# Moving the arena of a two-block transformer kernel by 128 bytes in every SBUF partition

## The reference

```python
# first block, depth 2
x = x + window_gqa_sink(h, w_qkv_a, w_out_a, sink_a)       # layer 0: windowed attention
x = x + dilated_mixture_attention(h, w_qkv_b, w_out_b)     # layer 1: three dilated groups
x = x + swiglu(h, w_gate, w_up, w_down)                    # after each: 1024 -> 2816 -> 1024
# second block, depth 2, on x (512 tokens) and a context y (256 tokens)
f_in, f_gate, g_u, g_v, g_gate, c_q, c_kv, k_rope, a_gate = _split_in(h @ w_in)
x = x + gate * (jnp.concatenate([fx, gx, ox], axis=-1) @ w_out[l])
```

## The kernel before, in words

| tile | address before | past a multiple of 256 |
|---|---|---|
| `w_lo`, `w_hi`, `x`, `y`, `ident`, `ones` | 16,512 (`w_lo`), 32,896 (`w_hi`) ... | 128 |
| `rows`, `sq` | 76,480 and 81,600 | 192 |
| first tile of the arena (`h_hi` and others) | 87,744 | 192 |
| all moving and stationary fp32r activation tiles (`h`, `a`, `b`, `f0m`, `f1m`, `l_hx`, `l_hy`, `l_h`, `l_m`, each `_hi` and `_lo`) | in the arena | 192 |
| `l_tm`, `l_gu`, `l_fg` | in the arena | 128 |

## Time and profile before

### The profile page before, as it was taken

How to read it: one execution, slowest core, us unless ns; L and a number is a source line. 1 busy time by engine, 2 the same in 40 slices (tenths; PEclk the granted TensorE clock), 3 DMA queues, 4 the chain that set the end, 5 groups by cost and what they waited for, 6 DMA issues and landing times.

```text
span 2251.5 us, 31279 instructions
## 1 busy us (share of the span) xinstructions
PE 2217.8 (99%) x13114; PEld 1795.1 (80%) x13114; DVE 998.9 (44%) x1519; ACT 832.7 (37%) x1291; POOL 735.1 (33%) x339
## 2 busy tenths in 40 slices
PE   9999999999999999999999999999999999999999
PEld 7778888888889888888778888887885667886677
DVE  5655555621222232223366555445204673541672
ACT  6544333233233343334453333333224432333531
POOL 3116444455432332323164444443220101332102
PEclk9999999999999999999999999999999999999999
DMA  4113444432322222122034444433110001322002
GB/s 147 40 47 112 140 141 147 152 103 94 116 84 67 67 66 75 66 73 68 30 103 144 150 147 141 134 100 122 57 65 33 1 1 38 131 75 80 1 1 75
DMA packets 54587, 193.36 MB, mean 86 GB/s; under 512 B 6832, under 2 KB 8112, under 8 KB 53552
## 3 DMA queue, kind: packets, MB, share of 16 engines
q1 hardware_dynamic: 43056, 153.72, 20.8%
q10 hardware_dynamic: 11392, 37.65, 4.4%
HBM read 189.24 MB, written 2.10 MB: 85 GB/s over the span
## 4 chain that ended last, share of the span: by engine, by line
PE 88%; DVE 3%; ACT 1%; issue 1%; DVEq 0%; DMA 0%; POOL 0%; POOLq 0%
PE ps L174 21%; PE ps L176 20%; PE ps L175 20%; PE ps L2523 4%; PE ps L177 3%; PE ps L179 3%; PE ps L178 3%; PE ps L2555 2%; PE ps L1052 2%; PE ps L1078 2%; PE ps L2535 2%; PE ps L1063 1%; PE ps L1919 1%; DVE dvS L1111 0%; DMA w_raw<-in_wstream 0%
## 5 line engine op out<-in xcount | busy, mean ns | idle before, releaser
L246 POOL TENSOR_TENSOR w_lo<-w_raw,w_hi 128x1024 fp32r<-128x1024 f32 x282 | 681.7, 2419 | 1390.4 <-ACT w_hi L164 1390.4
L174 PE MATMUL ps<-h_hi,w_hi 128*128 128x512 f32 x1168 | 469.9, 402 | 4.6 <-DVE w_lo L288 2.1
L164 ACT ACTIVATE w_hi<-w_raw 128x1024 fp32r<-128x1024 f32 x284 | 299.4, 1057 | 438.0 <-DMA w_raw<-in_wstream 436.7
L176 PE MATMUL ps<-h_hi,w_lo 128*128 128x512 f32 x1168 | 458.1, 392 | 0.0
L175 PE MATMUL ps<-h_lo,w_hi 128*128 128x512 f32 x1168 | 454.6, 389 | 0.0
L174 PEld LDWEIGHTS ps<-h_hi,w_hi 128*128 128x128 f32 x1168 | 219.5, 188 | 52.4 <-issue 4.0
L176 PEld LDWEIGHTS ps<-h_hi,w_lo 128*128 128x128 f32 x1168 | 219.3, 188 | 50.9
L175 PEld LDWEIGHTS ps<-h_lo,w_hi 128*128 128x128 f32 x1168 | 219.6, 188 | 45.5 <-issue 0.7
L1255 ACT ACTIVATE sq<-sq,dnm 128x768 f32<-128x768 f32 x64 | 59.4, 930 | 184.3 <-DVE dnm L1161 184.3
L177 PE MATMUL ps<-w_hi,h_hi 128*128 128x256 f32 x416 | 117.0, 281 | 3.2 <-DVE dvS L1111 3.2
L178 PE MATMUL ps<-w_lo,h_hi 128*128 128x256 f32 x416 | 115.2, 277 | 0.0
(11 more groups left out here) (323 smaller groups left out, 4141.0 us busy)
## 6 DMA issues: line engine op xcount, KB each, us to landing
w_raw<-in_wstream SPq DMA_DIRECT2D x283, 512.0 KB, 3.4
f0mod_rows<-in_wmod ACTq DMA_DIRECT2D x24, 512.0 KB, 4.2
f1mod_rows<-in_wmod ACTq DMA_DIRECT2D x24, 512.0 KB, 4.5
l_dft<-in_dft ACTq DMA_DIRECT2D x4, 1024.0 KB, 6.9
out<-x SPq DMA_DIRECT2D x8, 256.0 KB, 3.6
x<-in_x SPq DMA_DIRECT2D x3, 512.0 KB, 7.0
l_wuq<-in_wuq ACTq DMA_DIRECT2D x2, 768.0 KB, 6.7
dist<-in_dist ACTq DMA_DIRECT2D x1, 1152.0 KB, 6.4
```

Of the source, the lines that this page charges most:

```text
L164: self.A.activation(self.w_hi[:, n % RING, :], self.w_raw[:, n % RING, :], ACT.Copy).then_inc(self.w_high, 1)
L174: T.matmul(out, wh, ah, start=start, stop=False)
L176: return T.matmul(out, wl, ah, start=False, stop=stop)
L246: G.tensor_tensor(c.w_lo[:, n % RING, :], c.w_raw[:, n % RING, :], c.w_hi[:, n % RING, :].bitcast(F32), ALU.subtract).then_inc(c.w_low, 1)
```

## The change

The arena begins 128 bytes later: at 87,872 in place of 87,744, which is 64 past a multiple of 256. Everything placed by `ctx`, or at a sum of arena offsets, moves by the same 128 bytes: the fp32r activation tiles go from 192 to 64 past a multiple of 256, `l_tm`, `l_gu` and `l_fg` from 128 to 0. What is allocated ahead of the arena (the ring of weights, `x`, `y`, `rows`, `sq`) stays. No instruction is added, removed, reshaped or moved in the order of any engine, and no wait changes.

```diff
-        self.top = self.offset = (nc.sbuf_base + 31) // 32 * 32
+        self.top = self.offset = (nc.sbuf_base + 31) // 32 * 32 + 128
```

## The result

The changed kernel is slower: 2276.33 us median of 4 runs (2275.58 to 2279.34) against 2251.4 us (with one run more than in the table above), a ratio of 1.0112 (95% interval 1.0095 to 1.013), or 25 us. The profiled execution took 2276.8 us with a span of 2275.5 us, 24.0 us more than before. The forecast, no change, was wrong; the time is where the slower rival put it.

The account below looks back on a forecast made before the run. TensorE's pace from one matmul to the next was taken to bound the kernel, not waits or data transfers. Six terms of 0 left the span at 2251.5 us, forecast 2251.2 us, range 2226 to 2281.

Parts of the forecast that it names:

- the slower rival: Moving slices at 64 past 256 fall to the pace of those at 128: 27.2 us, 2278.4 us; chance 0.25.
- Items 1 to 4: Orders and waits, other engines on arena tiles, DMAs landing in the arena, plain fp32 matmuls: each taken as 0.
- item 4: Plain fp32 matmuls, 0.430 us from start to start: change taken as 0.
- Item 5: 512-column fp32r matmuls moving from the arena, 1984 triples: taken as no change; upper bound 0.700 us a triple.
- block "kr": Stationary slices start at 128 and 0 past 256 in turn, triples keep 0.70 and 0.69 us: evidence for no change.
- Rows 6: Profile rows of L177, weights moving from 128 past 256 over arena tiles: 0.700 us a triple.
- rows 5: Profile rows of the down product, moving slices at 192 past 256: 0.686 us a triple, durations 394, 388 and 392 ns.
- Item 6: fp32r matmuls with 256 columns, seen at 0.343 and 0.357 us a triple: 0 to +5.8 us, taken as 0.
- the whole stall: Rival: the matmul stream gets faster by its whole stall; chance 0.06, left out of the forecast's range.

Follow-up runs that it names:

- the map: Kernel without the reference's work, 96 matmuls a line at chosen starts; 512 columns: 226.9, 229.1, 232.4, 233.3 ns at differences 0, 64, 128, 192.
- the two maps: The map and a second such kernel, with alternating starts and column counts mixed; 256 columns at difference 192 took 113.4 and 117.7 ns in the second.

## Why the prediction was wrong

**The bound was right.** The pace at which TensorE takes fp32r matmuls sets the time, 1984 triples of L174 first among them. Of the 26 us that the distances account for, 24 are there. The steadiness that the prediction read from the earlier trace rows stands in the single distances as well: in the down product of the kernel before all 529 lie between 225 and 232 ns, 231 or 232 after each start of L174, 225 or 226 after L175, 229 or 230 after L176. From 440 to 561 us VectorE was busy 30.78 us, ScalarE 39.01 and GpSimd 64.14, and the DMA share went from 0.25 to 0.47 by stretches of 20 or 21 us.

**Items 1 to 4 held.** No wait moved, the other engines and DMAs stayed under their cover, and plain fp32 matmuls have 0.429 us a record at every difference tried. The granted clock at the earlier trace rows was 1.00. The 0 of item 4 was the author's estimate; no row of the kernel before varies an address there, and it is the map that shows it, with L98 to L101 alike.

**Item 5 failed, and it was the choice of value, not the bounds.** The upper bound, 0.700 us a triple and 27.2 us in all, is what happened: the down product has exactly this pace, and over all stages the 512-column distances are worth 24 us. "I take no change" rested on block "kr": alternating stationary starts left its triples at 0.70 and 0.69 us, hence no relation between the streams with a period of 256 bytes. There is one. The map shows why "kr" was too weak a witness: with 32 columns loaded the four differences lie within 1 ns (230.7 to 231.7), with 128 columns 6.4 ns apart. The prediction named this weakness and then kept the conclusion. The second support, that 192 and 64 are alike modulo 128 while 128 is not, looked for the cause in the moving slice's own place. Rows 6 and rows 5 had held the right variable all along: with the difference written beside each, they read "64: 0.686, 192: 0.700", and the change turns the one into the other. Two rows for one variable, and the change to be forecast was the value of the second.

**The slower rival was right in its price and its size, wrong in its mechanism.** It made the moving slice's place in 256 bytes the cause. By that, L177, whose moving slices stay, keeps 0.700 us; it went to 0.686. And the kernel with everything 128 bytes later would have been slow; it is not. That its price fits is in part luck: it took 0.700 us from the row that stood at difference 192, and 192 is what the change makes at L174. How much of a matmul's 228.8 ns is stall no run shows, and so none shows the whole stall to which the forecast gave 0.06; what the runs showed in its place is 226.8 ns, the shortest mean pace of any line of the two maps with 512 columns (L59 and L75 of the first), 2.0 ns below.

**Item 6 was half right.** That addresses modulo 256 alone don't fix the pace with 256 columns, and that more than one pattern exists, both maps confirm. Taking 0 was too low: L177's 1,223 distances cost 3.5 us of the 5.8 allowed.

**What the addresses do.** The runs show 226.9 to 233.3 ns at starts that are all multiples of 64. What the map measures is an effect of the one slice's address on the other's stream, 6.4 ns of some 230; whether it arises at the memory or in the array, no run here shows.

## What to carry to other kernels

Where a stream of fp32r matmuls bounds a kernel, read the distance of starts and write the difference of the moving and the stationary start addresses, modulo 256 bytes, beside each form: moving both tiles together changed nothing here (2251.26 us), moving one alone gave triples of 0.680 to 0.700 us in the down product, 3% apart. For 512 columns let both start at the same residue (226.9 ns). For 256 columns 192 was the best of the four, but not reliably (113.4 and 117.7 ns), so read the distances after it. And an observation that excludes an effect must be made in the form that bears the time: a block with a quarter of the load was the wrong witness.

## What the runs showed of the hardware that was not expected

- fp32r matmuls, 128 loaded columns, 512 moving: 226.9, 229.1, 232.4 and 233.3 ns from start to start at differences of 0, 64, 128 and 192 bytes, whatever the absolute starts in steps of 64 bytes; 128 had 233.3 behind other work.
- With 256 columns the order is another: 117.8 ns at 64, 120 at 0, and at 192 two steady paces, 113.4 and 117.7, for the same two starts.
- With starts between the steps of 64, 512 columns have two paces for the same two starts as well: 226.8 and 236.5 ns at moving 112 over stationary 128.
- Plain fp32 matmuls on the same tiles show none of it: 0.429 us a record at all four differences.
